# Preparing the sample attention between heads of the prompt attention's last two tiles

## What is computed

```python
def nsa_core(q, qpos, gates, kv_cmp, gather_sel, kv_band, band_pos, n_blocks):
    qs = q * (HEAD_DIM ** -0.5)
    p_c = masked_softmax(jnp.einsum('bqhgd,bchd->bqhgc', qs, kv_cmp[:, :, 0]), m_c)   # block keys
    o_c = jnp.einsum('bqhgc,bchd->bqhgd', p_c.astype(dt), kv_cmp[:, :, 1])
    ...                                                       # blocks ranked, the top 16 selected
    p_s = masked_softmax(jnp.einsum('bqhgd,bqhkd->bqhgk', qs, kv_sel[..., 0, :]), m_s)
    ...
    p_w = masked_softmax(jnp.einsum('bqhgd,bkhd->bqhgk', qs, kv_band[:, :, 0]), m_w)  # window
    ...
    return gates[..., 0:1] * o_c + gates[..., 1:2] * o_s + gates[..., 2:3] * o_w
```

## Time and profile before

| what | before |
|---|---|
| median of 3 runs | 1126.96 us (1126.88 to 1131.83) |
| the profiled execution's own time | 1131.71 us |
| its span in the trace | 1130.0 us |
| `attend_prompt` in the trace | about 289 to 772 us |
| `tail` in the trace | 772.6 us to the end |
| TensorE busy | 978.9 us (87%) |
| VectorE busy | 605.0 us (54%) |
| ScalarE busy | 413.3 us (37%) |

### The profile page before, as it was taken

How to read it: one execution, slowest core, us unless ns; L and a number is a source line. 1 busy time by engine, 2 the same in 40 slices (tenths; PEclk the granted TensorE clock), 3 DMA queues, 4 the chain that set the end, 5 groups by cost and what they waited for, 6 DMA issues and landing times. The chain is left out here.

```text
span 1130.0 us, 16674 instructions
## 1 busy us (share of the span) xinstructions
PE 978.9 (87%) x5935; PEld 830.2 (73%) x5935; DVE 605.0 (54%) x1394; ACT 413.3 (37%) x892; POOL 242.5 (21%) x197
## 2 busy tenths in 40 slices
PE   3999999999688888998898889987577998998976
PEld 3999999999687877777788778764244666664654
DVE  4531110474333567886345668875666566567640
ACT  4432211120323455665134446662332343433311
POOL 3029599994100000000000500000420000000001
PEclk9899999999879999999799989996866999999888
DMA  6227535340511110000110124004205244462310
GB/s 202 72 75 230 184 106 179 117 163 21 164 39 45 32 33 7 2 1 8 32 39 27 42 64 124 1 1 173 75 26 160 80 134 135 125 177 66 91 36 28
DMA packets 106677, 93.73 MB, mean 83 GB/s; under 512 B 21102, under 2 KB 99811, under 8 KB 104483
## 3 DMA queue, kind: packets, MB, share of 16 engines
q1 hardware_dynamic: 84946, 58.65, 17.3%
q10 hardware_dynamic: 19344, 17.25, 5.1%
q0 software_dynamic: 2304, 16.78, 4.3%
HBM read 78.16 MB, written 18.61 MB: 86 GB/s over the span
## 5 line engine op out<-in xcount | busy, mean ns | idle before, releaser
L1265 DVE TENSOR_TENSOR pt_lo<-ps,pt_hi 128x512 fp32r<-128x512 f32 x132 | 90.9, 688 | 67.9 <-ACT pt_hi L1181 67.7
L588 PE MATMUL ps<-w_hi,h_hi 128*128 128x264 f32 (+5 forms) x432 | 125.7, 291 | 1.0 <-DVE h_lo L457 1.0
L588 PE MATMUL ps<-w_lo,h_hi 128*128 128x264 f32 (+5 forms) x432 | 124.6, 289 | 0.0
L588 PE MATMUL ps<-w_hi,h_lo 128*128 128x264 f32 (+5 forms) x432 | 124.5, 288 | 0.0
L1181 ACT ACTIVATE pt_hi<-ps 128x512 fp32r<-128x512 f32 x132 | 78.5, 597 | 102.3 <-PE ps L1088 101.5
L1261 DVE TENSOR_REDUCE least<-ps 128x1 f32<-128x640 f32 (+7 forms) x128 | 90.0, 703 | 15.7 <-PE ps L1075 14.5
L465 DVE TENSOR_TENSOR w_lo<-w_raw,w_hi 128x1024 fp32r<-128x1024 f32 (+2 forms) x12 | 29.9, 2495 | 122.0 <-ACT w_hi L366 122.0
L1036 PE MATMUL ps<-h_hi,wr_hi 128*128 128x362 f32 (+1 forms) x192 | 74.8, 389 | 22.4 <-DVE stage_b L1236 18.9
L313 POOL TENSOR_TENSOR chunk<-chunk 128x1024 f32<-128x1024 f32 (+2 forms) x46 | 81.9, 1781 | 3.6
L588 PEld LDWEIGHTS ps<-w_hi,h_hi 128*128 128x128 f32 (+1 forms) x432 | 81.3, 188 | 1.8 <-ACT h_hi L357 1.0
L588 PEld LDWEIGHTS ps<-w_lo,h_hi 128*128 128x128 f32 (+1 forms) x432 | 81.4, 188 | 0.0
(11 more groups left out here) (374 smaller groups left out, 2425.0 us busy)
## 6 DMA issues: line engine op xcount, KB each, us to landing
kv_pages<-in_cache_slc_kv SPq DMA_DIRECT2D x256, 64.0 KB, 1.9
shared<-in_x_prompt SPq DMA_DIRECT2D x8, 512.0 KB, 3.6
w_raw<-in_w_in SPq DMA_DIRECT2D x8, 512.0 KB
wr_raw<-in_w_in SPq DMA_DIRECT2D x8, 512.0 KB, 3.9
kv_window<-in_cache_win_kv SPq DMA_DIRECT2D x4, 1024.0 KB, 5.6
wo_raw<-in_w_out SPq DMA_DIRECT2D x8, 512.0 KB, 8.4
out<-in_cache_win_kv SPq DMA_DIRECT2D x1, 4032.0 KB
x_row<-in_x_prompt ACTq DMA_DIRECT2D x7, 512.0 KB, 4.3
```

Of the source, the lines that this page charges most:

```text
L588: mm = nc.tensor.matmul(out, lhs, rhs, start=(k == 0 and i == 0), stop=(k == KD - 1 and i == 2))
L1265: nc.vector.tensor_tensor(pt_lo[:, t % PTS, :], ps[:, turn_bank(x, t), :], pt_hi[:, t % PTS, :].bitcast(F32), ALU.subtract).then_inc(s_ptl, 1)
```

## The change

The prologue of `tail` becomes four steps of `attend_prompt`'s list, placed in the last two tiles of the second key head (UNITS is 32, so they fall in units 29 and 30): s_stage after head 0 of unit 29, s_query after head 2 of unit 29, s_keys after head 1 of unit 30, s_gates after head 3 of unit 30. Their PSUM is bank 7, under the same `spare()` rule; the queries are staged in the buffer `q_st`, which the prompt no longer needs then. Four tiles move into the region that outlives the block. In `tail` the prologue keeps only the three memsets.

```diff
@@ in attend_prompt, schedule()
+                early = {(3, 0): "s_stage", (3, 2): "s_query", (2, 1): "s_keys", (2, 3): "s_gates"}
+                if (UNITS - u, y) in early:
+                    yield early[UNITS - u, y], 0, 0
...
     uses = [(k, x) for what, x, _ in steps
-            for k in {"query": ("q",), "c_scores": ("cs",), "c_turn": ("ct",), "c_values": ("co",), "output": ("z",)}.get(what, ())]
+            for k in {"query": ("q",), "c_scores": ("cs",), "c_turn": ("ct",), "c_values": ("co",), "output": ("z",), "s_query": ("sq",), "s_keys": ("sk",)}.get(what, ())]
...
+        q_nat = q_st[0:NS]
@@ TensorE
+                    elif what == "s_query":
+                        out = spare(("sq", x))
+                        pe.wait_ge(s_qst, NKV * NT + 1)
+                        for g in range(NG):
+                            nc.tensor.transpose(out[:, g * NS:(g + 1) * NS],
+                                                q_nat[:, g, :, :].rearrange("p h d -> p (h d)"), ident[0:NS, 0:NS])
+                        for n, c in enumerate((K_SLC, K_WIN)):
+                            mm = nc.tensor.transpose(out[:, (NG + n) * NS:(NG + n + 1) * NS], pn[:, c:c + ROW],
+                                                     ident[0:NS, 0:NS])
+                        mm.then_inc(s_sp, 1)
+                    elif what == "s_keys":
+                        out = spare(("sk", x))
+                        for h in range(2):
+                            mm = nc.tensor.transpose(out[:, h * P:(h + 1) * P], kc[:, h, 0, :], ident[:, :])
+                        mm.then_inc(s_sp, 1)
@@ ScalarE
+                    elif what == "s_gates":
+                        act.wait_ge(L.s_gl, 16 * DB)
+                        nc.scalar.activation(L.gates[:, :, :], L.gates[:, :, :], ACT.Exp, scale=-1.0
+                                             ).then_inc(s_gate, 1)
@@ VectorE
+                    elif what == "s_stage":
+                        dve.wait_ge(s_sp, place["q", NKV * NT - 1] + 1)
+                        for g in range(NG):
+                            last = nc.vector.tensor_copy(
+                                q_nat[:, g, :, :],
+                                pq[0:NS, NT, :].rearrange("p (h g d) -> p h g d", h=NKV, g=NG)[:, :, g, :])
+                        last.then_inc(s_qst, 1)
+                    elif what == "s_query":
+                        dve.wait_ge(s_sp, place["sq", x] + 1)
+                        dve.wait_ge(L.s_const, 1)
+                        for h in range(NKV):
+                            r = slice(h * HD, (h + 1) * HD)
+                            nc.vector.tensor_copy(L.q_bd[r, :, h, :, :],
+                                                  ps[r, 7, 0:NG * NS].rearrange("p (g b t) -> p b g t", g=NG, b=DB))
+                        nc.vector.tensor_copy(L.k_new[:], ps[:, 7, NG * NS:(NG + 2) * NS].rearrange(
+                            "p (n c) -> p n c", n=2)).then_inc(s_spr, 1)
+                    elif what == "s_keys":
+                        dve.wait_ge(s_sp, place["sk", x] + 1)
+                        nc.vector.tensor_copy(L.kcT_s[:], ps[:, 7, 0:2 * P].rearrange("p (a b) -> p a b", a=2)
+                                              ).then_inc(s_spr, 1)
+                        dve.wait_ge(L.s_const, 1)
+                        v.did(nc.vector.tensor_reduce(
+                            L.causal8[:, :], L.causal[:, :].rearrange("p (a t) -> p t a", t=DS), AX, ALU.add))
+                        dve.wait_ge(L.s_small, 80)
+                        v.did(nc.vector.tensor_scalar(L.gcol[:, 1:2], L.gcol[:, 0:1], 0.5, None, ALU.mult))
+                        v.wait()
+                        v.did(nc.vector.tensor_scalar(L.wpen[:, :], L.causal8[:, :], NEG, None, ALU.mult))
+                    elif what == "s_gates":
+                        dve.wait_ge(s_gate, 2)
+                        v.did(nc.vector.tensor_scalar(L.gates[:, :, :], L.gates[:, :, :], 1.0, None, ALU.add))
+                        v.wait()
+                        v.did(nc.vector.reciprocal(L.gates[:, :, :], L.gates[:, :, :]))
@@ in tail, TensorE
-                pe.wait_ge(s_qn, 1)
-                for g in range(NG):
-                    mm = nc.tensor.transpose(ps[:, SC, g * NS:(g + 1) * NS],
...
-                pe.wait_ge(s_qbd, 1)
-                pe.wait_ge(s_kce, 1)
@@ in tail, ScalarE
-                act.wait_ge(L.s_gl, 16 * DB)
-                nc.scalar.activation(gates[:, :, :], gates[:, :, :], ACT.Exp, scale=-1.0).then_inc(s_gate, 1)
@@ in tail, VectorE
-                dve.wait_ge(L.s_const, 1)
-                dve.wait_ge(L.s_small, 80)
-                nc.vector.memset(aT[:, :], 1.0)
+                nc.vector.memset(aT[:, :], 1.0).then_inc(s_ones, 1)
                 nc.vector.memset(state[:, :], 0.0)
                 v.did(nc.vector.memset(prob[:, PAST + NS:], 0.0))
-                nc.vector.tensor_scalar(gcol[:, 1:2], gcol[:, 0:1], 0.5, None, ALU.mult).then_inc(s_gcol, 1)
...
```

More of the change, by code:

```diff
@@ L1362, in __init__ @@
         self.mark = at("mark", [P, 1])
+        self.k_new, self.kcT_s = at("k_new", [P, 2, NS]), at("kcT_s", [P, 2, P])
+        self.causal8, self.wpen = at("causal8", [P, DS]), at("wpen", [P, DS])
         assert self.end <= self.base + 8 * KD * TOK
@@ L1788, in tail @@
         q_bd = L.q_bd
-        k_new = sb("k_new", [P, 2, NS])
-        kcT = sb("kcT_s", [P, 2, P])
+        k_new, kcT_s, causal8, wpen = L.k_new, L.kcT_s, L.causal8, L.wpen
         gates, same, causal, own, own_pen, kvsel = L.gates, L.same, L.causal, L.own, L.own_pen, L.kvsel
-        causal8 = sb("causal8", [P, DS])
         new_pen = sb("new_pen", [P, DB, DS])
-        wpen = sb("wpen", [P, DS])
         c_s = sb("cs_s", [P, 2, DB, NPG])
@@ L1987, in _ @@
                         ge(pe, s_comb, 3 * x)
-                        nc.tensor.matmul(ps[:, V, 0:2 * P], q_pair(x), kcT[:, :, :].rearrange("p a b -> p (a b)"),
+                        nc.tensor.matmul(ps[:, V, 0:2 * P], q_pair(x), kcT_s[:, :, :].rearrange("p a b -> p (a b)"),
                                          start=True, stop=True).then_inc(s_csc, 1)
```

39 lines of the change are left out of this document (4 added, 35 removed).

## The result

The changed kernel takes 1138.64 us in the median of its first 5 runs (1132.86 to 1140.68) and 1135.62 us in that of 12 later ones (1131.05 to 1140.69, e9 below). Its ratio to the kernel before is 1.0076, interval 1.0039 to 1.0113, and in the second comparison 1.0070, 1.0043 to 1.0098. So it is slower by 0.7%, and both medians lie above the forecast's 1129.0 and its range of 1125 to 1133.

What follows compares the result with a forecast made beforehand. TensorE's list was taken to set the pace in the prompt's last tiles, with a bare chain of about 4 us at the seam. +4.0 waits and work, +1.7 clock, -3.7 head start gave +2.0 us: 1129.0, range 1125 to 1133.

Steps and rivals of the forecast that it cites:

- The waits: In attend_prompt's moved steps, waits and work cost 2.6 for s_stage and s_query, 1.3 for s_keys, 0.1 for s_gates: +4.0 us.
- TensorE's idle before the six turns: At s_query in unit 29, TensorE waits for VectorE's c_pT copy, without work from 730.5 to 733.7, 3.2 us.
- that before the block keys: At s_keys, the block keys' two turns wait for VectorE's "scaled"; TensorE idles over 1 us, step costs +1.3.
- the gates' delay: At s_gates, VectorE's "least" starts 1.1 us late, but a 1.06 us idle behind it takes nearly all: +0.1.
- the bounds of 3.4 and 5.4: Bounds on the +4.0 us of waits and work: short turns with 1.1 for s_keys, or long ones with 1.6.
- I add +1.7; bounds 0 (no fall) and 3.4: TensorE's clock falls once behind s_query's wait, costing 1.7 us; 3.4 if s_keys' wait makes a second fall.
- All else follows from the chain. I carry 3.7 to the end.: At the seam, removing the prologue starts tail 3.7 us sooner (bounds 2.6 to 4.1), kept to the end.
- rival 3: In tail, a transfer timed from the seam or ScalarE's list loses the 3.7 us head start: 1132.7, chance 0.14.
- last sign of being wrong: The forecast is wrong if tail, from its barrier to the end, changes by other than 3 to 4 us.
- theory B: Rival theory set for the experiments: the loss arises in tail, by the move as such.
- A: Theory set for the experiments: TensorE's two waits cost, and the clock falls behind them, for more than forecast.
- C: Rival theory set for the experiments: VectorE's added work in the heads costs, wherever TensorE waits.

Runs made afterwards that it cites:

- e9: The changed kernel measured again beside the kernel before: 1135.62 us median of 12 runs, mean 1135.7.
- e2: The changed kernel with unread matmuls filling TensorE's two waits, 12 ahead of s_query's and 4 ahead of s_keys': 1131.16 us, ratio 1.0028.
- e1: The kernel before with only two waits added on TensorE, where s_query and s_keys would make it wait, no work moved: 1140.62 us, ratio 1.0132.
- e10: The kernel of e1 measured again, against the kernel before: 1134.54 us, ratio 1.0043.
- e5: The kernel of e1 with unread matmuls ahead of each wait, 12 and 4: 1128.16 us, ratio 1.0038 to the kernel before.
- e3: The changed kernel with its four steps at other heads of units 30 and 31, where the bank is free: 1129.95 us, ratio 1.0019.
- e7: The kernel of e4 with TensorE's start in tail held back about 1.5 us by an added VectorE memset: 1126.37 us, ratio 0.9999.
- e11: The kernel before with only the second wait of e1, behind the output of unit 28: 1129.35 us, ratio 1.0012.
- e6: The kernel before with only the first wait of e1, behind c_turn of unit 29: 1131.87 us, ratio 1.0047.
- e4: The changed kernel with its four steps moved to the sparse end of the prompt attention, behind the last heads: 1126.64 us, ratio 0.9988.
- e13: The changed kernel without its four steps anywhere, constants standing in their tiles: 1129.87 us, ratio 1.0022 to the kernel before.
- e14: The kernel before, prologue where it was, with unread matmuls at the sparse end and 30 in tail's longest idle: 1126.36 us, ratio 0.9992.
- e8: The kernel of e4 with unread matmuls in TensorE's idles at the sparse end of attend_prompt: 1124.40 us, ratio 0.9972.
- e12: The kernel of e8 with 30 more unread matmuls in tail's idle of 15.7 us: 1123.18 us, ratio 0.9966.

## Why the prediction was wrong

**The waits were right.** TensorE's idle before the six turns was 2.91 us (forecast 3.2), that before the block keys 1.13 (1.3), and the gates' delay went into the cover of the earlier trace rows. e2, where the clock is held, has the size: at the "least" behind the gates the waits and the work have cost 3.98 us, against the +4.0 of the forecast. In the changed kernel the same "least" is 7.1 us late, and in e9 5.6: the forecast's 4.0, and 3.1 and 1.6 for two falls and one. Two slips in the working did no harm: the scores of head 3 at 734.3 with 2.1 us of work behind them put c_values at 736.4, not 736.0 (e2 shows it 2.8 us late, as was written), and the bounds of 3.4 and 5.4 come out of their own terms at about 3.7 and 5.2.

**The term that was mis-sized: "I add +1.7; bounds 0 (no fall) and 3.4".** The filling of the two waits returned 5.5 us (mean of the changed kernel's 17 runs, 1136.1, less e2) and 6.3 (e1 with e10, less e5; 5.8 without the run of 1145.44). The stretches agree: 60.4 and 57.3 us (e9) against 50.5, less the 4.0 of waits and work, leave 5.9 and 2.8 to the clock. The forecast priced one fall rightly (0.57 over 732 to 736 is 1.7 us) and allowed for a second. It didn't ask what happens at the next place where TensorE is sparsely fed: in the changed kernel, in e9, e1 and e10 the clock also fell in the sparse end, from 758 to 766 on, where it held in the trace of before until 771.5. How firmly that fall belongs to the waits is open: it came in e2, e3, e7 and e11 too, and not in e5, e6, e4 and e13. e4 and e7 are the same program up to the seam, and it came in one of them: chance has a part in it. Behind the second wait it came in one trace of five. By the runs, the clock behind the waits makes about two thirds of the +8.4.

**The step that failed: "All else follows from the chain. I carry 3.7 to the end."** The head start was there, 4.2 us, for 3.7 forecast. It was carried for some 150 us and then lost. e13, which has it and nothing else, is 1.9 us slower than before in the mean; its interval, 0.9996 to 1.0049, leaves room for no change, but not for a gain of 3.7. This is rival 3 in its outcome, to which I gave 0.14, but by neither of its mechanisms: no transfer and no list of ScalarE's took more than 0.8 us of it in e13 (the table there), and TensorE's own clock took the rest, from 155 us behind the memset on. The forecast's own last sign of being wrong came true as well: `tail` was to get 3 to 4 us shorter, and took 0.7 longer. From the memset on, the six traces with the prologue (leaving out e14 with its fillers) take 357.1, 357.5, 357.5, 359.4, 359.7 and 360.1 us (mean 358.6), the six without it (leaving out e8 and e12 with their fillers in the sparse end, and e7 with its delay) 353.9, 356.2, 357.8, 357.9, 357.9 and 359.3 (mean 357.2). So the 4 us are worth 1.4 on average, with a spread of 5 between equal orders. The times are as unsteady: +1.9 in e13 and -1.4 in e4, which has the same order in `tail` and a stretch of the same length.

So the sum of the forecast, +4.0 + 1.7 - 3.7, should have read +4.0 for waits and work, 4.4 (the two stretches) to 5.5 (the filling) for the clock, and 0 to -1.4 for the head start. That makes +7.0 to +9.5, and the 17 runs give +8.4.

**The experiments' theory B** stands beside A, then: the waits' clock is the larger part, the lost head start the other. C is not the main cause: e1 has none of the work and loses as much. With the clock held the waits alone cost +2.7 in the mean (e5), so at most some 1.3 of the 4.0 are left to VectorE's added work. What stays open is whether the falls in `tail` come more often without the prologue. The one near 155 us behind the memset came in four of the six traces without it and in one of the six with it, the one near 250 in five and in three. e7 moved the start by 1.5 us and the times didn't tell; the traces are too few to separate a cause in the start's time from chance.

**Where the steps belong.** e4 shows that the same steps cost `attend_prompt` nothing where TensorE waits anyway. Whether other columns of bank 7 could take the turns without a wait wasn't tried.

The Trainium skill, "TensorE: Matmul & The Clock Gate", section "A second HAM failure mode: psum-queue depth-cycling", says that short idles between groups of matmuls, if they are frequent enough, make the clock swing between its two levels. The sparse end of the changed kernel agrees in kind: TensorE is busy 2.23 of 4 us over 762 to 766, and 0.52 is granted over 766 to 770. But e4, with TensorE busy 2.61 of 4 us over 757 to 761, has no fall before 769.7. By this rule the bound of the clock term would not have ended at two falls.

## What to carry to other kernels

A wait put on the engine that sets the pace costs itself once, and its clock may fall two or three times behind it (three times in the first trace of the changed kernel, twice in e9): price it at its length plus the work behind it at half rate, and look for the next sparse stretch that the delay will reach. Small work of preparation belongs where that engine already waits (e4), not behind the use of a buffer that has just been written, and where a wait has to be, matmuls that nobody reads can hold the clock (e2, e5), which pays only where TensorE sets the pace (not in e12). A head start of 4 us ahead of 350 us in which the clock comes and goes is not a gain until a run with nothing but the head start shows it (e13); and one pair of traces doesn't tell, since equal programs differ there by 5 us. Line the same instruction up in both traces to see where a gain is lost.

## What the runs showed of the hardware that was not expected

The same list of instructions from the memset on took between 353.9 us (e4) and 359.3 us (e13). All but some 0.5 us of the difference arises at the three places where e13's clock fell and e4's did not, or for less long. An idle of 2.5 to 2.9 us in the dense stretch brought the lower level in every trace that had it unfilled (the changed kernel twice, e1, e6, e10); one of 1.1 us brought it in the first trace of the changed kernel (0.57 over 742 to 746) and not in e9, e1, e10 and e11. The window of e11 there reads:

```profile
730.00:736.00 6.00, 4.65 (x29) 3.86 (x28) 4.63 (x8) 3.08 (x6) 0.00 (x0) 1.00 0.00 0
```

Some 50 matmuls of no use, added on TensorE, made the kernel no slower (e14, 1126.5 in the mean), and e12 with its 52 lies 2.1 us below e4, about the uncertainty. 24 us less at the lower level in `tail` (e12 against e8) shortened it by 0.5 us.
